# Two unused 64-byte buffers around the activations' low and high halves, in a two-layer decoder trunk on one core

## The chip, the core and the metric

The kernel runs on one core of one Trainium2 chip. The metric is the device time of one execution in microseconds (us); lower is better. A core has TensorE (PE for its matmuls, PEld for its weight loads), VectorE (DVE), ScalarE (ACT), GpSimd (POOL) and SyncE (SP, which here only issues DMAs), one on-chip memory of 128 partitions (SBUF) that all of them read, and PSUM, which holds the matmuls' sums.

## The reference

`x` is 256 tokens by 2048 features, float32. Two layers run one after the other, each followed by a SwiGLU feed-forward block of 5632 hidden features:

```python
c_act = silu(c)
for i in range(2):
    sh1, sc1, g1, sh2, sc2, g2 = split(c_act @ ada_w[i] + ada_b[i], 6)
    h = x * (1 + sc1) + sh1
    y = mixer_ab(h, ...) if i == 0 else mixer_cd(h, ...)
    x = layer_norm(ALPHA * x + (1 + g1) * y, ln1_g[i], ln1_b[i])
    h = x * (1 + sc2) + sh2
    y = (silu(h @ w_gate[i]) * (h @ w_up[i])) @ w_down[i]
    x = layer_norm(ALPHA * x + (1 + g2) * y, ln2_g[i], ln2_b[i])
```

`mixer_ab` is one input projection (2048 to 5136), gated DeltaNet heads beside S5 state-space groups, and an output projection; `mixer_cd` is an input projection (2048 to 6144), a short gated convolution beside differential attention, and an output projection. All weights are float32 and are read once from HBM, about 612 MB in all.

## The kernel before

**Products.** Every large matrix product is cut into weight units of 512 rows by 512 columns (1 MB). SP loads a unit into one of four slots of `w_raw` (line 896 issues it). ACT writes its rounded high part into `w_hi` (line 978), DVE subtracts to get the rest into `w_lo` (line 1262), each with two slots. The activations of a product are split the same way into two buffers: `act_hi` and `act_lo` for all products but the down projections, which take `hid_hi` and `hid_lo`. TensorE then runs three matmuls for each 128 rows: high times high, low times high, high times low, in the format fp32r.

**Two shapes.** In the narrow form (lines 1749, 1751, 1753) a 128x128 block of the weights is what TensorE loads as its stationary operand and 128x256 of the activations streams past it. The products `in0u`, `in0`, `glu`, `out0`, `in1a`, `in1b`, `out1` run so with `act_hi`/`act_lo`, 124 units; the down projections run so with `hid_hi`/`hid_lo`, 88 units. A unit is 16 blocks and 48 matmuls. In the wide form (lines 1741, 1743, 1745) a 128x128 block of the activations is stationary and 128x512 of the weights streams. The gate and up projections run so with `act_hi`/`act_lo`, 176 units of 24 matmuls. The narrow lines:

```python
pe.matmul(dst, whi[:, j % 2, kk, cols], hi[:, k], ...)
pe.matmul(dst, whi[:, j % 2, kk, cols], lo[:, k], ...)
last = pe.matmul(dst, wlo[:, j % 2, kk, cols], hi[:, k], ...)
```

**Order.** The products follow one another on all engines in the order `in0u`, `in0`, `glu`, then the DeltaNet rounds, `out0`, a layer norm, three pairs of up and down blocks, a layer norm, `in1a`, `in1b` (with the attention between its units), `out1`, a layer norm, three pairs of up and down blocks, a last layer norm. Beside them DVE sums the products `c_act @ ada_w` (line 1249) out of units that POOL's or SP's queue loads into `ada_units`; the last of these belongs to the first block of the second layer's up projection.

**Buffers.** `sb(name, shape)` takes the next free bytes of every partition, in the order of the lines, so a buffer's address is the sum of the sizes ahead of it. `shared([...])` takes space and gives it back at once, so that what comes next lies over it: `ada_first` (49152 bytes in each partition), used only at the start, lies over `w_lo`, `act_hi` and `act_lo`. The sizes in bytes of each partition, in order: `w_raw` 32768, `w_hi` 16384, `ada_units` 16384, `ada_acc` 4096, `xT` 16384, `w_lo` 16384, `act_hi` 16384, `act_lo` 16384, then from `mod` to `dn_small` 16 small buffers (columns of vectors, `ident`, `ones`, small weights) of 5824 together, then `y` 16384, `hid_hi` 16384, `hid_lo` 16384, `gate_t`, `gate_s`, `ln_stat`, and over the same space from `y` on the buffers of the S5, DeltaNet and attention stages.

```python
raw = sb("w_raw", [P, 4, UK, GROUP])
whi = sb("w_hi", [P, 2, UK, GROUP], F32R)
aw = sb("ada_units", [P, 2, UK, GROUP])
acc = sb("ada_acc", [P, 2, GROUP])
xT = sb("xT", [P, KT, L])
wlo = sb("w_lo", [P, 2, UK, GROUP], F32R)
ahi = sb("act_hi", [P, KT, L], F32R)
alo = sb("act_lo", [P, KT, L], F32R)
```

Of the kernel before, what the change touches and what calls it, by code (L numbers as in the profile page):

```python
# [12 lines left out]
P = 128  # L13
# [106 lines left out]
def build(nc, x, c, ada_w, ada_b, ln1_g, ln1_b, ln2_g, ln2_b, ffn_w_gate, ffn_w_up, ffn_w_down,  # L120
# [10 lines left out]
    with ctx:  # L131
        def sb(name, shape, dt=F32):
            return ctx.enter_context(nc.sbuf_tensor(name, shape, dt))
# [4 lines left out]
        def shared(layout):  # L138

            with ExitStack() as s:  # L140
                return [s.enter_context(nc.sbuf_tensor(n, shape, F32 if not dt else dt[0])) for n, shape, *dt in layout]
# [7 lines left out]

        (first6,) = shared([("ada_first", [P, FIRST_SLOTS - 2, UK, GROUP])])  # L150
        wlo = sb("w_lo", [P, 2, UK, GROUP], F32R)
        ahi = sb("act_hi", [P, KT, L], F32R)
        alo = sb("act_lo", [P, KT, L], F32R)
        mod = sb("mod", [P, DEPTH * N_ADA])
        adab = sb("ada_b_cols", [P, DEPTH * N_ADA])
        lnc = sb("ln_cols", [P, 4 * DEPTH * KT])
# [1873 lines left out]
```

## Time and profile before

| | us |
|---|---|
| median of 3 runs | 2971.28 |
| lowest and highest | 2968.68, 2972.24 |
| the profiled execution, its own time | 2971.53 |
| its span, first to last instruction | 2968.1 |

Over the span PE is busy 89%, its weight loads 80%, DVE 71%, ACT 40%, POOL 8%; the mean granted clock is 0.914 of full speed. A profile row gives the time from the start of the span in us; a busy share says how long an engine was occupied, not that it ran at its peak: matmuls are pipelined, so one that is listed with 0.28 us may be followed by the next after 0.12 us. The rate is therefore read from the starts.

### The profile page before, as it was taken

The page shows a single profiled execution, that of the slowest core. Times are in us where ns is not written, and L with a number is a line of the kernel's source. Part 1 is how long each engine was busy: PE and PEld are TensorE (multiplying, and loading weights), DVE is VectorE, ACT ScalarE, POOL GpSimd, SP SyncE. Part 2 cuts the span into 40 slices and gives each one's busy share as a digit, 9 for nine tenths or more (in the row PEclk, how much of TensorE's full clock was granted, in tenths as well). Part 3 has the DMA queues.
Part 4 walks back from the last instruction along what each step waited for, and adds up shares of the span by engine and source line. Part 5 has one row for each costly group of instructions (what it writes and reads, how often), then busy time and mean ns, then how long its engine had stood idle before and what let it go on. Part 6 is the DMA issues. An engine that isn't in the chain of part 4 may idle for free.

```text
span 2968.1 us, 43237 instructions
## 1 busy us (share of the span) xinstructions
PE 2640.9 (89%) x16620; PEld 2373.7 (80%) x16620; DVE 2116.8 (71%) x2742; ACT 1200.1 (40%) x1509; POOL 233.2 (8%) x274
## 2 busy tenths in 40 slices
PE   1299999566679899999999989999889999999998
PEld 1298887455569788988898889999878898889887
DVE  7778887666668777777777788756887755555556
ACT  0135554322214544334434445355345434443444
POOL 0012221111120000000000101100000000000000
PEclk6599999665569999999999999999999999999998
DMA  9853333122347488788778859945657755555552
GB/s 339 274 199 114 120 122 119 66 99 99 113 149 275 161 285 284 269 278 285 279 271 281 286 182 324 335 151 169 243 172 270 268 191 192 190 192 189 195 184 85
DMA packets 288724, 615.90 MB, mean 208 GB/s; under 512 B 22572, under 2 KB 23107, under 8 KB 288323
## 3 DMA queue, kind: packets, MB, share of 16 engines
q1 hardware_dynamic: 253762, 479.64, 47.7%
q0 software_dynamic: 34816, 134.23, 12.9%
q8 instruction: 103, 1.69, 0.2%
q14 instruction: 43, 0.34, 0.0%
HBM read 611.73 MB, written 2.10 MB: 207 GB/s over the span
## 4 chain that ended last, share of the span: by engine, by line
PE 76%; issue 11%; DVE 7%; POOL 2%; ACT 1%; DMA 1%; SPq 1%; DVEq 0%; POOLq 0%; ACTq 0%
PE groups L1749 13%; PE groups L1753 12%; PE groups L1751 12%; PE groups L1741 11%; PE groups L1745 10%; PE groups L1743 10%; PE pc L1918 2%; DVE ada_acc L1249 1%; PE pm L1716 1%; PE pb L1907 1%; POOL dn_mb L620 1%; SPq L896 1%; DVE w_lo L1262 1%; DMA ada_units<-in_ada_w_dram 1%; DVE ada_acc L1591 1%
## 5 line engine op out<-in xcount | busy, mean ns | idle before, releaser
L1262 DVE TENSOR_TENSOR w_lo<-w_raw,w_hi 128x1024 fp32r<-128x1024 f32 x773 | 938.5, 1223 | 575.6 <-ACT w_hi L978 571.6
L978 ACT ACTIVATE w_hi<-w_raw 128x1024 fp32r<-128x1024 f32 x776 | 817.5, 1059 | 1262.0 <-PE groups L1753 600.0
L1749 PE MATMUL groups<-act_hi,w_hi 128*128 128x256 f32 x1968 | 572.3, 291 | 43.1 <-DVE act_lo L1392 13.3
L1741 PE MATMUL groups<-w_hi,act_hi 128*128 128x512 f32 x1408 | 554.5, 394 | 25.5 <-DVE act_lo L1392 25.5
L1751 PE MATMUL groups<-act_lo,w_hi 128*128 128x256 f32 x1968 | 563.8, 286 | 0.0
L1753 PE MATMUL groups<-act_hi,w_lo 128*128 128x256 f32 x1968 | 563.5, 286 | 0.0
L1745 PE MATMUL groups<-w_lo,act_hi 128*128 128x512 f32 x1408 | 550.6, 391 | 0.0
L1743 PE MATMUL groups<-w_hi,act_lo 128*128 128x512 f32 x1408 | 550.4, 391 | 0.0
L1249 DVE SCALAR_TENSOR_TENSOR ada_acc<-ada_units,c_act,ada_acc 128x512 f32<-128x512 f32 x600 | 468.2, 780 | 26.3 <-DMA ada_units<-in_ada_w_dram 9.1
L1749 PEld LDWEIGHTS groups<-act_hi,w_hi 128*128 128x128 f32 x1968 | 385.2, 196 | 56.2 <-issue 39.8
L1749 PE MATMUL groups<-hid_hi,w_hi 128*128 128x256 f32 x1392 | 388.1, 279 | 0.0
L1753 PE MATMUL groups<-hid_hi,w_lo 128*128 128x256 f32 x1392 | 386.7, 278 | 0.0
L1751 PE MATMUL groups<-hid_lo,w_hi 128*128 128x256 f32 x1392 | 386.7, 278 | 0.0
L1751 PEld LDWEIGHTS groups<-act_lo,w_hi 128*128 128x128 f32 x1968 | 385.3, 196 | 0.2
L1753 PEld LDWEIGHTS groups<-act_hi,w_lo 128*128 128x128 f32 x1968 | 384.7, 195 | 0.0
L1741 PEld LDWEIGHTS groups<-w_hi,act_hi 128*128 128x128 f32 x1408 | 266.2, 189 | 82.2 <-DVE act_lo L1392 28.0
L1745 PEld LDWEIGHTS groups<-w_lo,act_hi 128*128 128x128 f32 x1408 | 265.8, 189 | 55.9
L1743 PEld LDWEIGHTS groups<-w_hi,act_lo 128*128 128x128 f32 x1408 | 266.3, 189 | 54.6
L1751 PEld LDWEIGHTS groups<-hid_lo,w_hi 128*128 128x128 f32 x1392 | 262.7, 189 | 0.1
L1749 PEld LDWEIGHTS groups<-hid_hi,w_hi 128*128 128x128 f32 x1392 | 261.6, 188 | 0.1
L1753 PEld LDWEIGHTS groups<-hid_hi,w_lo 128*128 128x128 f32 x1392 | 261.7, 188 | 0.0
L889 POOL DMA_DIRECT2D ada_units<-in_ada_w_dram x128 | 96.2, 751 | 1585.1 <-DVE ada_acc L1249 1443.8
(385 smaller groups left out, 2251.5 us busy)
## 6 DMA issues: line engine op xcount, KB each, us to landing
ada_units<-in_ada_w_dram POOLq DMA_DIRECT2D x128, 1024.0 KB, 6.4
w_raw<-in_ffn_w_gate_dram SPq DMA_DIRECT2D x88, 1024.0 KB, 5.2
w_raw<-in_ffn_w_up_dram SPq DMA_DIRECT2D x88, 1024.0 KB, 5.2
w_raw<-in_ffn_w_down_dram SPq DMA_DIRECT2D x88, 1024.0 KB, 5.1
w_raw<-in_cd_w_in_dram SPq DMA_DIRECT2D x48, 1024.0 KB, 6.0
ada_units<-in_ada_w_dram SPq DMA_DIRECT2D x40, 1024.0 KB, 5.1
w_raw<-in_ab_w_in_dram SPq DMA_DIRECT2D x40, 1024.0 KB, 5.0
ada_first<-in_ada_w_dram SPq DMA_DIRECT2D x24, 1024.0 KB, 9.5
```

Source lines behind the costliest of these rows:

```text
L620: done(pool.tensor_tensor(mb[:], m[:], lm[:, k].unsqueeze(1).broadcast_to([P, 4, P]), ALU.mult))
L889: engine.dma_start(aw[:, j % 2], src[UK * P * j:UK * P * (j + 1), bass.ds(col, GROUP)] .rearrange("(k p) n -> p k n", p=P)).then_inc(lande ...
L978: act.activation(whi[:, half, k], raw[:, slot, k], ACT.Copy).then_inc(hi_done, 1)
L1249: last = dve.scalar_tensor_tensor(acc[:, b], unit[:, kk], cact[:, k:k + 1], acc[:, b], ALU.mult, ALU.add)
L1262: dve.tensor_tensor(wlo[:, half, k], raw[:, slot, k], whi[:, half, k].bitcast(F32), ALU.subtract).then_inc(lo_done, 1)
L1741: pe.matmul(dst, hi[:, k, rows], whi[:, j % 2, kk], start=(k == 0), stop=False, skip_group_check=True)
L1743: pe.matmul(dst, lo[:, k, rows], whi[:, j % 2, kk], start=False, stop=False, skip_group_check=True)
L1745: last = pe.matmul(dst, hi[:, k, rows], wlo[:, j % 2, kk], start=False, stop=(k == UK * p["units"] - 1), skip_group_check=True)
L1749: pe.matmul(dst, whi[:, j % 2, kk, cols], hi[:, k], start=(q == 0 and kk == 0 and n % 2 == 0), stop=False, skip_group_check=True)
L1751: pe.matmul(dst, whi[:, j % 2, kk, cols], lo[:, k], start=False, stop=False, skip_group_check=True)
L1753: last = pe.matmul(dst, wlo[:, j % 2, kk, cols], hi[:, k], start=False, stop=(q == p["units"] - 1 and kk == UK - 1), skip_group_check=True)
L1918: last = pe.matmul(pc[cols, 0:L], s5w[:, t, 2 + m, cols], turned[:, c], start=(m == 0 and c == 0), stop=(m == 1 and c == 1))
```

## The change

Two buffers of 16 float32 in each partition are allocated and never written or read. `act_gap` stands ahead of `act_hi`, `act_end` behind `act_lo`. No instruction, wait, loop or transfer is added or removed.

```diff
         wlo = sb("w_lo", [P, 2, UK, GROUP], F32R)
+        sb("act_gap", [P, 16])
         ahi = sb("act_hi", [P, KT, L], F32R)
         alo = sb("act_lo", [P, KT, L], F32R)
+        sb("act_end", [P, 16])
         mod = sb("mod", [P, DEPTH * N_ADA])
```

So `act_hi` and `act_lo` lie 64 bytes further on, and `mod` and all that follows it, `y`, `hid_hi` and `hid_lo` among them, 128 bytes. The buffers from `w_raw` to `w_lo` stay where they are.

## Rows read from the trace of the kernel before

**Rows 1.** Top of the page: span, busy time and share of each engine.

```profile
span 2968.1 us, 43237 instructions
PE 2640.9 (89%) x16620; PEld 2373.7 (80%) x16620; DVE 2116.8 (71%) x2742; ACT 1200.1 (40%) x1509; POOL 233.2 (8%) x274
```

**Rows 2.** The chain that ended last, shares of the span by engine, by line.

```profile
PE 76%; issue 11%; DVE 7%; POOL 2%; ACT 1%; DMA 1%; SPq 1%; DVEq 0%; POOLq 0%; ACTq 0%
PE groups L1749 13%; PE groups L1753 12%; PE groups L1751 12%; PE groups L1741 11%; PE groups L1745 10%; PE groups L1743 10%; PE pc L1918 2%; DVE ada_acc L1249 1%; PE pm L1716 1%; PE pb L1907 1%; POOL dn_mb L620 1%; SPq L896 1%; DVE w_lo L1262 1%; DMA ada_units<-in_ada_w_dram 1%; DVE ada_acc L1591 1%
```

**Rows 3.** Groups of instructions: shapes, count | busy us, mean ns | idle before.

```profile
L1749 PE MATMUL groups<-act_hi,w_hi 128*128 128x256 f32 x1968 | 572.3, 291 | 43.1 <-DVE act_lo L1392 13.3 <-DVE act_lo L1511 11.1 <-DVE act_lo L1675 7.3
L1741 PE MATMUL groups<-w_hi,act_hi 128*128 128x512 f32 x1408 | 554.5, 394 | 25.5 <-DVE act_lo L1392 25.5
L1749 PE MATMUL groups<-hid_hi,w_hi 128*128 128x256 f32 x1392 | 388.1, 279 | 0.0
...
L1262 DVE TENSOR_TENSOR w_lo<-w_raw,w_hi 128x1024 fp32r<-128x1024 f32 x773 | 938.5, 1223 | 575.6 <-ACT w_hi L978 571.6
L1392 DVE TENSOR_TENSOR act_lo<-y,act_hi 128x1024 fp32r<-128x1024 f32 x9 | 11.0, 1221 | 2.4 <-ACT act_hi L1089 2.4
```

**Rows 4.** Timeline of PE, product in1a, narrow form: start, us, instruction; first and last.

```profile
1869.75 0.28 PE L1749 MATMUL groups<-act_hi,w_hi 128*128 128x256 f32 x1
...
1874.91 0.28 PE L1751 MATMUL groups<-act_lo,w_hi 128*128 128x256 f32 x1
```

**Rows 5.** Timeline of PE, up projection, wide form, first and last.

```profile
2499.76 0.39 PE L1745 MATMUL groups<-w_lo,act_hi 128*128 128x512 f32 x1
...
2509.96 0.39 PE L1745 MATMUL groups<-w_lo,act_hi 128*128 128x512 f32 x1
```

**Rows 6.** Timeline of PE, down projection of the second layer, narrow form, first and last.

```profile
2419.74 0.28 PE L1749 MATMUL groups<-hid_hi,w_hi 128*128 128x256 f32 x1
...
2424.95 0.28 PE L1751 MATMUL groups<-hid_lo,w_hi 128*128 128x256 f32 x1
```

**Rows 7.** Timeline of PE, down projection of the first layer, narrow form, first and last.

```profile
1239.73 0.28 PE L1753 MATMUL groups<-hid_hi,w_lo 128*128 128x256 f32 x1
...
1244.91 0.28 PE L1751 MATMUL groups<-hid_lo,w_hi 128*128 128x256 f32 x1
```

**Rows 8.** Timeline of PE, start of in1a, at the granted clock of rows 9, first and last.

```profile
1764.57 0.41 PE L1749 MATMUL groups<-act_hi,w_hi 128*128 128x256 f32 x1
...
1766.49 0.41 PE L1749 MATMUL groups<-act_hi,w_hi 128*128 128x256 f32 x1
```

**Rows 9.** Stretches: length, busy us of each engine (instructions), granted clock, DMA share, GB/s.

```profile
1764.50:1767.00 2.50, 2.50 (x14) 2.50 (x13) 1.67 (x6) 2.08 (x4) 0.00 (x0) 0.50 0.00 0
...
1325.00:1360.00 35.00, 35.00 (x156) 28.97 (x155) 29.31 (x32) 14.81 (x16) 3.00 (x4) 1.00 0.78 265
1870.00:1895.00 25.00, 25.00 (x211) 25.00 (x210) 23.46 (x29) 9.61 (x10) 2.99 (x4) 1.00 1.01 374
...
2400.00:2430.00 30.00, 30.00 (x267) 30.00 (x266) 15.03 (x15) 11.71 (x12) 0.00 (x0) 1.00 0.55 177
2500.00:2520.00 20.00, 20.00 (x90) 16.57 (x89) 9.50 (x8) 8.20 (x8) 0.00 (x0) 1.00 0.60 203
205.00:495.00 290.00, 284.60 (x1920) 234.03 (x1920) 241.06 (x334) 151.88 (x252) 67.89 (x64) 0.99 0.34 116
1240.00:1270.00 30.00, 30.00 (x258) 30.00 (x257) 23.55 (x27) 11.00 (x11) 2.40 (x4) 1.00 0.83 285
```

**Rows 10.** The chain in order of time inside in1a: start, us, what.

```profile
1844.00 8.08 DMA ada_units<-in_ada_w_dram
...
1855.95 8.20 DMA ada_units<-in_ada_w_dram
```

## Prediction

> **What bounds the kernel now.** I read the top of the page first: PE is busy 89% of the span [rows 1]. The chain that ended last confirms it as the bound: 76% of it is PE, and 68% (13+12+12+11+10+10) are the six matmul lines of the products [rows 2]. Busy time does not give the rate of a pipelined engine, so I read starts. Four stretches, each with PE busy all through at a granted clock of 1.00, that is 2.4 GHz [rows 9]:
>
> - narrow, activations in `act_hi`/`act_lo`: 44 matmuls, so 43 steps in 1874.91-1869.75 = 5.16 us, 120.0 ns each [rows 4];
> - wide, same activations: 46 matmuls, 45 steps in 10.20 us, 226.7 ns [rows 5];
> - narrow, `hid_hi`/`hid_lo`: 47 matmuls, 46 steps in 5.21 us, 113.3 ns [rows 6];
> - the same in the first layer: 45 matmuls, 44 steps in 5.18 us, 117.7 ns [rows 7].
>
> At 2.4 GHz 256 columns take 106.7 ns and 512 take 213.3. So a matmul with `act` costs 13.3 ns beyond its columns in either shape, though the shapes differ twofold in length and swap which operand is loaded and which streams. With `hid` it costs 6.7 or 11.0. At a granted clock of 0.50 (1.2 GHz) [rows 9] 10 matmuls of the narrow form with `act` stand 1.92/9 us = 213.3 ns apart, exactly 256 columns [rows 8]: there nothing is added. The excess is a cost of feeding the array at full speed, with one weight load to each matmul, and it depends on which buffer holds the activations. The readers of `act` and `hid` run the same three lines with the same waits.
>
> **What differs between act and hid: the address.** From the sizes, `act_hi` lies 16384+16384+4096+16384+16384 = 69632 bytes behind `w_hi`, a whole number (136) of 512 bytes; rows, blocks and slots of both are multiples of 512 apart, so the loaded and the streamed operand always start on the same place of 512 bytes. `hid_hi` lies 69632+32768+5824+16384 = 124608 behind `w_hi`, 243 times 512 and 192. With 192 = 128+64, `hid` is not on the same place of any 128 bytes. `w_lo` is a multiple of 512 from `w_hi`, and the low halves are 16384 from the high ones.
>
> **The change, part by part.** It adds no instruction and no transfer; all it can do is through these distances. `act` moves from 0 to 64 (modulo 512) and `hid` from 192 to 320. Modulo 128 that is 0 to 64 for `act`, and 64 before and after for `hid`. If two streams that start on the same place collide most, and the pattern repeats every 128 bytes, `act` comes to where `hid` is and `hid` stays.
>
> Price of a matmul: `hid` runs at 113.3 or 117.7 ns [rows 6, 7], 6.7 or 2.3 below 120.0. I take the middle, 4.5, where `act` runs long undisturbed, since `hid` shows both in just such stretches. Bounds are 0 and 6.7.
>
> - Narrow with `act`: 3x1968 = 5904 matmuls [rows 3]. I take off some 250, an estimate, for the runs at 1.2 GHz behind pauses, like that of [rows 8], where nothing is added. `in1a` has 1152 of them at 374 GB/s and a DMA share of 1.01 [rows 9], and its chain already waits twice for `ada_units` [rows 10]: a faster PE waits there for DMA, so I take 0. That leaves 4500. Of these `in0` and `in1b` (56 units, 2688) are cut up, a unit or two at a time, by the S5 and attention matmuls between them; in 205 to 495 us PE's 1920 matmuls are `in0`'s 1536 and 384 others [rows 9]. Here I take the smaller 2.3, since nothing shows what such short pieces settle to: 6.2 us. The other 1800 at 4.5: 8.1 us. Together 14.3 us; bounds 0 and 30.
> - Wide: 3x1408 = 4224 matmuls [rows 3], in long runs. The excess is the same 13.3 ns there, so I take the same 4.5: 19.0 us; bounds 0 and 28.2. The trace has no wide matmul at another distance, so this is the less certain half. What could cap it: a unit of 24 would take 5.32 us instead of 5.44. DVE, busy 29.31 of 35 us [rows 9], and DMA at 265 to 285 GB/s [rows 9] both have more room than the 2% needed.
> - Down projections: 4176 matmuls, 0. If half of them run at 117.7 now and all fell to 113.3, that would give 2088 x 4.3 = 9 us; that is a bound.
> - DVE and ACT: `w_lo` (operands 32768 apart, 0 modulo 512) takes 1223 ns, `act_lo` (operands not on the same place) 1221 for the same elements [rows 3]. So addresses cost DVE nothing, and I take nothing for all moved buffers, vector columns and `ada_first` (in place) included. Waits in layer norms, DeltaNet and attention stay as they are.
>
> Sum: 14.3+19.0 = 33.3 us. The profiled execution took 2971.5 us, 2968.1 of span and 3.4 around it, and is 0.2 from the median shown. 2971.5-33.3 = 2938.
>
> The Trainium skill speaks against any of this: "TensorE: Matmul & The Clock Gate", section "Step-by-step: what each phase is for", says that PE has two independent read ports, so that loading the next weights takes no read bandwidth from the running matmul, and "SBUF — State Buffer", section "Who interferes with whom", that PE waits on nobody. By that the distances would not matter and the time stays at 2971. The first page's section "Back-to-back issue gap" gives N/2.4 + 2.5 ns for one matmul alone, 109.2 and 215.8; the trace is above both with either buffer, by rows 4 to 7.
>
> **The rivals.**
>
> *Nothing moves (2971).* Rows 6 and 7 have the same lines, shape and addresses and still differ by 4.3 ns, so a part of the spacing comes from how loads and matmuls fall into step, not from addresses. If the remaining difference to `act` is also that, or if the pattern repeats every 64 bytes (both 0 and 192 are then the same), the change is nothing. Against it: the difference of buffer goes one way in every pair of [rows 4] against [rows 6, 7], and the wide form, with other lengths and the operands swapped, has the same 13.3 ns [rows 5] as the narrow [rows 4].
>
> *Only one shape gains.* Narrow alone: 2971.5-14.3 = 2957. Wide alone: 2971.5-19.0 = 2952. For it: which operand moves is swapped, so a distance of +64 is -64 in the other shape.
>
> *Only the step at 117.7 is reached.* 2.3 ns on 8724 matmuls: 20 us, 2951.
>
> *Slower: hid loses its place (2990).* If the pattern is longer than 128 bytes, 320 modulo 512 need not be as good as 192. Should the down projections take `act`'s 120.0 while `act` keeps its own, 4176 x 4.5 ns = 19 us are added. It decides as soon as `hid` loses more than `act` gains: at a loss of 4.5 on `hid`, when `act` gains less than 19 us / 8724 = 2.2 ns a matmul. The like for `act`, a distance worse than the same place, has no row for it; doubled to 6.7 more it would cost 58 us.
>
> **How the numbers follow.** Both shapes gain, 2904 to 2951: 0.45. Only one gains, 2952 to 2957: 0.15. Nothing: 0.20. Slower: 0.17. The rest, 0.03, is a small gain near 2963. The range reaches from the best bound (30+28.2+9 = 67, 2904, cut to 2910, since that needs every matmul at its best) to 2973, just past no change, which leaves out the slower cases. The likeliest case alone is 2912 to 2951. 0.2% is 6 us, about what a measurement of this kernel can tell from no change: faster 0.62, same 0.21, slower 0.17.
>
> **What the next profile would show.** Right: spacing of the narrow form in `in1b`, `out1` and of the wide form falls from 120.0 and 226.7 to 113-118 and 220-224, with `hid` as before and the counts of [rows 3] unchanged; `in1a` as long as before, with more DMA in its chain; durations on DVE and ACT unchanged. Wrong: `act` at 120.0 and 226.7 as before, or the down projections' stretches [rows 6, 7] at 120. The step I trust least is the wide form's 4.5 ns.

## The result and the profile after

The changed kernel takes 3003.5 us (median of 4 runs) against 2971.7 (4 runs): ratio 1.0102, interval [1.0088, 1.0117]. It is slower by 1.0%, about 32 us; forecast were 2938 us and a range of 2910 to 2973. The profiled execution has a span of 2999.0 us, 30.9 more than before [rows 1].

Top of the page, then the line of the chain by source line. Two lines were inserted, so a line of before has a number higher by two: L1743, L1745, L1747 are the wide form, L1751, L1753, L1755 the narrow one.

```profile
span 2999.0 us, 43237 instructions
PE 2668.6 (89%) x16620; PEld 2371.6 (79%) x16620; DVE 2116.9 (71%) x2742; ACT 1199.5 (40%) x1509; POOL 233.0 (8%) x274
...
PE groups L1751 12%; PE groups L1753 12%; PE groups L1755 12%; PE groups L1743 11%; PE groups L1745 11%; PE groups L1747 11%; PE pc L1920 2%; DVE ada_acc L1251 1%; PE pm L1718 1%; PE pb L1909 1%; DMA ada_units<-in_ada_w_dram 1%; SPq L898 1%; POOL dn_mb L622 1%; DVE w_lo L1264 1%; DVE ada_acc L1593 1%
```

The instructions are the same in number, DVE and ACT are as busy as before to 0.6 us, the granted clock is 0.914 in both. PE is busy 27.7 us longer. Groups of the page, as in [rows 3]:

```profile
L1264 DVE TENSOR_TENSOR w_lo<-w_raw,w_hi 128x1024 fp32r<-128x1024 f32 x773 | 937.8, 1223 | 604.0 <-ACT w_hi L980 601.9
...
L1751 PE MATMUL groups<-act_hi,w_hi 128*128 128x256 f32 x1968 | 566.1, 288 | 45.3 <-DVE act_lo L1394 13.7
L1743 PE MATMUL groups<-w_hi,act_hi 128*128 128x512 f32 x1408 | 561.8, 399 | 22.0 <-DVE act_lo L1394 22.0
...
L1751 PE MATMUL groups<-hid_hi,w_hi 128*128 128x256 f32 x1392 | 389.9, 280 | 0.0
```

The mean duration of a narrow matmul with `act` fell from 291 to 288 ns, that of a wide one rose from 394 to 399, that with `hid` from 279 to 280. DVE still takes 1223 ns for a piece; its idle time before `w_lo` rose from 575.6 to 604.0 us, nearly all of it (601.9) waiting for ACT, whose own longest wait is for PE. The rate shows in the starts. Four stretches of PE's timeline (start, duration, instruction; first and last), with 45, 44, 45 and 44 matmuls:

```profile
1884.80 0.28 PE L1755 MATMUL groups<-act_hi,w_lo 128*128 128x256 f32 x1
...
1889.98 0.28 PE L1753 MATMUL groups<-act_lo,w_hi 128*128 128x256 f32 x1
...
2519.74 0.39 PE L1747 MATMUL groups<-w_lo,act_hi 128*128 128x512 f32 x1
...
2529.78 0.39 PE L1743 MATMUL groups<-w_hi,act_hi 128*128 128x512 f32 x1
...
2429.77 0.28 PE L1751 MATMUL groups<-hid_hi,w_hi 128*128 128x256 f32 x1
...
2434.95 0.28 PE L1755 MATMUL groups<-hid_hi,w_lo 128*128 128x256 f32 x1
...
1244.84 0.28 PE L1753 MATMUL groups<-hid_lo,w_hi 128*128 128x256 f32 x1
...
1249.90 0.28 PE L1755 MATMUL groups<-hid_hi,w_lo 128*128 128x256 f32 x1
```

- narrow with `act`: 5.18 us / 44 = 117.7 ns, was 120.0 [rows 4];
- wide with `act`: 10.04 / 43 = 233.5, was 226.7 [rows 5];
- `hid`, second layer: 5.18 / 44 = 117.7, was 113.3 [rows 6];
- `hid`, first layer: 5.06 / 43 = 117.7, as before [rows 7].

Where the 31 us went, by the time from the first to the last start of each stretch of products, in both traces:

| products | before, us | after, us | difference |
|---|---|---|---|
| up, six blocks (wide) | 1001.7 | 1026.4 | +24.7 |
| down, six blocks (`hid`) | 495.7 | 507.1 | +11.4 |
| `in0u` to `glu` (narrow, `act`) | 385.7 | 384.1 | -1.6 |
| `out0` (narrow, `act`) | 96.5 | 95.0 | -1.5 |
| `in1a` to `out1` (narrow, `act`) | 423.5 | 418.5 | -5.0 |
| sum | | | +28.0 |

The other 3 us of the 31 lie outside the products: the first one starts 1.4 us later, and the DeltaNet stretch between `glu` and `out0` is 1.6 us longer.

### The profile page after: what moved, and what is told of

The parts are those of the page before. It is cut to its first block, busy times and chain, and to the rows that moved or that the text cites. A ratio compares the mean times of both kernels' runs of the same rounds, so it can differ in the third digit from the quotient of the medians.

```text
span 2999.0 us, 43237 instructions
## 1 busy us (share of the span) xinstructions
PE 2668.6 (89%) x16620; PEld 2371.6 (79%) x16620; DVE 2116.9 (71%) x2742; ACT 1199.5 (40%) x1509; POOL 233.0 (8%) x274
## 4 chain that ended last, share of the span: by engine, by line
PE 77%; issue 11%; DVE 7%; POOL 1%; ACT 1%; DMA 1%; SPq 1%; DVEq 0%; POOLq 0%; ACTq 0%
PE groups L1751 12%; PE groups L1753 12%; PE groups L1755 12%; PE groups L1743 11%; PE groups L1745 11%; PE groups L1747 11%; PE pc L1920 2%; DVE ada_acc L1251 1%; PE pm L1718 1%; PE pb L1909 1%; DMA ada_units<-in_ada_w_dram 1%; SPq L898 1%; POOL dn_mb L622 1%; DVE w_lo L1264 1%; DVE ada_acc L1593 1%
## 5 line engine op out<-in xcount | busy, mean ns | idle before, releaser
L1264 DVE TENSOR_TENSOR w_lo<-w_raw,w_hi 128x1024 fp32r<-128x1024 f32 x773 | 937.8, 1223 | 604.0 <-ACT w_hi L980 601.9
L1751 PE MATMUL groups<-act_hi,w_hi 128*128 128x256 f32 x1968 | 566.1, 288 | 45.3 <-DVE act_lo L1394 13.7
L1743 PE MATMUL groups<-w_hi,act_hi 128*128 128x512 f32 x1408 | 561.8, 399 | 22.0 <-DVE act_lo L1394 22.0
L1745 PE MATMUL groups<-w_hi,act_lo 128*128 128x512 f32 x1408 | 558.3, 397 | 0.0
L1747 PE MATMUL groups<-w_lo,act_hi 128*128 128x512 f32 x1408 | 558.1, 396 | 0.0
L1753 PE MATMUL groups<-act_lo,w_hi 128*128 128x256 f32 x1968 | 557.5, 283 | 0.0
L1755 PE MATMUL groups<-act_hi,w_lo 128*128 128x256 f32 x1968 | 557.2, 283 | 0.0
L1751 PEld LDWEIGHTS groups<-act_hi,w_hi 128*128 128x128 f32 x1968 | 378.4, 192 | 58.4 <-issue 42.0
L1751 PE MATMUL groups<-hid_hi,w_hi 128*128 128x256 f32 x1392 | 389.9, 280 | 0.0
L1753 PE MATMUL groups<-hid_lo,w_hi 128*128 128x256 f32 x1392 | 389.7, 280 | 0.0
L1755 PE MATMUL groups<-hid_hi,w_lo 128*128 128x256 f32 x1392 | 388.4, 279 | 0.0
L1753 PEld LDWEIGHTS groups<-act_lo,w_hi 128*128 128x128 f32 x1968 | 378.5, 192 | 0.2
L1755 PEld LDWEIGHTS groups<-act_hi,w_lo 128*128 128x128 f32 x1968 | 377.9, 192 | 0.0
L1743 PEld LDWEIGHTS groups<-w_hi,act_hi 128*128 128x128 f32 x1408 | 265.8, 189 | 88.5 <-DVE act_lo L1394 24.5
L1747 PEld LDWEIGHTS groups<-w_lo,act_hi 128*128 128x128 f32 x1408 | 265.6, 189 | 66.0
L1745 PEld LDWEIGHTS groups<-w_hi,act_lo 128*128 128x128 f32 x1408 | 265.8, 189 | 63.6
L1751 PEld LDWEIGHTS groups<-hid_hi,w_hi 128*128 128x128 f32 x1392 | 261.7, 188 | 0.1
L1753 PEld LDWEIGHTS groups<-hid_lo,w_hi 128*128 128x128 f32 x1392 | 261.3, 188 | 0.1
L1755 PEld LDWEIGHTS groups<-hid_hi,w_lo 128*128 128x128 f32 x1392 | 260.4, 187 | 0.0
```

The costliest lines, as they stand in the source:

```text
L1264: dve.tensor_tensor(wlo[:, half, k], raw[:, slot, k], whi[:, half, k].bitcast(F32), ALU.subtract).then_inc(lo_done, 1)
L1743: pe.matmul(dst, hi[:, k, rows], whi[:, j % 2, kk], start=(k == 0), stop=False, skip_group_check=True)
L1745: pe.matmul(dst, lo[:, k, rows], whi[:, j % 2, kk], start=False, stop=False, skip_group_check=True)
L1747: last = pe.matmul(dst, hi[:, k, rows], wlo[:, j % 2, kk], start=False, stop=(k == UK * p["units"] - 1), skip_group_check=True)
L1751: pe.matmul(dst, whi[:, j % 2, kk, cols], hi[:, k], start=(q == 0 and kk == 0 and n % 2 == 0), stop=False, skip_group_check=True)
L1753: pe.matmul(dst, whi[:, j % 2, kk, cols], lo[:, k], start=False, stop=False, skip_group_check=True)
```

## The experiments

The theory that I tested, D: the distance between the buffer of the activations and the buffers of the weights, modulo some period, sets the spacing of the product's matmuls. Rivals: what else moved (S), the place in the memory itself (A), chance of timing (P). The kernels of experiments 1 to 12 and 16 are the one before with unused buffers of other sizes; "act at 64" means 64 bytes more than before between `w_hi` and `act_hi`, and `hid` is named by its distance modulo 512. Beside each timeline I give a mean: the mean spacing over all neighbouring matmuls of that kind in the trace, without pauses and without stretches at 1.2 GHz (over 5400 narrow with `act`, over 4100 with `hid`, over 4000 wide), in the order narrow with `act`, `hid`, wide; it is good to about 0.1 ns. For the kernel before these means are 119.9, 115.0 and 226.8, for the changed one 117.4, 117.8 and 233.3.

**1. The buffers behind alone.**

```diff
         alo = sb("act_lo", [P, KT, L], F32R)
+        sb("act_end", [P, 32])
```

> act stays at distance 0 (modulo 512) from w_hi, hid and all small buffers move 128 bytes as in the changed kernel. Theory D (the distance of an activation buffer from the weights' buffers sets the spacing of its own matmuls): hid at 117.7 ns in all stretches, act at 120.0 and 226.7 as before; 4176 x 2.8 ns = +12 us, about 2983 us. Theory S (the moved small buffers, or the program as a whole, slow it): the wide form loses its 6.6 ns here too, about 3000 us. Theory P (the spacing is how loads and matmuls fall into step by chance of timing): nothing, 2971 us.

Measured 1.0036 [1.0018, 1.0054], 2981.4 us. `hid` at 320, then the wide form:

```profile
2419.78 0.28 PE L1752 MATMUL groups<-hid_lo,w_hi 128*128 128x256 f32 x1
...
2424.96 0.28 PE L1750 MATMUL groups<-hid_hi,w_hi 128*128 128x256 f32 x1
...
2499.76 0.39 PE L1744 MATMUL groups<-w_hi,act_lo 128*128 128x512 f32 x1
...
2509.96 0.39 PE L1744 MATMUL groups<-w_hi,act_lo 128*128 128x512 f32 x1
```

45 matmuls in 5.18 us are 117.7 ns where [rows 6] had 113.3; 46 in 10.20 us are 226.7, as before. The means are 119.9, 117.3, 226.9. `hid` slows when it moves by itself, by about a third of the whole loss (down blocks 505.0 us, 9.3 more than before), though not in all stretches: in two of the six blocks 4 of 11 pieces of 48 steps still stood at 113.3. S falls for the wide form.

**2. act alone.**

```diff
+        sb("act_gap", [P, 16])
         ahi = sb("act_hi", [P, KT, L], F32R)
         alo = sb("act_lo", [P, KT, L], F32R)
+        sb("act_end", [P, 112])
```

> act at distance 64, hid at 192+512 = 704, which is 192 modulo 512. Theory D with a period of 512 or less: act as in the changed kernel (117.7 narrow, 233.3 wide), hid as before the change (113.3 and 117.7, mean 115.0); -12+28 = +16 us, about 2987 us. If hid stays at 117.7 throughout, the period is longer than 512 or hid's state is not its distance: about 2999 us.

1.0109 [1.0086, 1.0131], 32 us by the ratio (26 by the medians) against the 16 forecast for an undisturbed `hid`; it is the other branch, 2999 us, that came. 45 wide matmuls took 10.27 us, 233.4 ns, and 45 of `hid` 5.18 us, 117.7 ns, where [rows 6] had 113.3:

```profile
2509.64 0.39 PE L1743 MATMUL groups<-w_hi,act_hi 128*128 128x512 f32 x1
...
2519.91 0.39 PE L1747 MATMUL groups<-w_lo,act_hi 128*128 128x512 f32 x1
...
2429.74 0.28 PE L1753 MATMUL groups<-hid_lo,w_hi 128*128 128x256 f32 x1
...
2434.92 0.28 PE L1751 MATMUL groups<-hid_hi,w_hi 128*128 128x256 f32 x1
```

The means are 117.8, 117.1, 233.3. `act` behaves as in the changed kernel. But `hid`, at its old distance, ran at 117.7 most of the time: the down blocks took 504.6 us, 8.9 more than before, nearly as much as in experiment 1. So at 192 it has two states, 113.3 and 117.7, and which one holds is not given by its distance. As both also occur at 320 (experiment 1), the two distances differ for `hid` in how often each state holds, not in the values.

**3. Both 512 further on** (`act_gap` of 128 elements, no other).

> act and hid both move 512 bytes, so both keep their place modulo 512. Theory D with a period of 512 or less: no change, 2971 us, 120.0, 226.7 and 115.0 ns. Theory S: as slow as the changed kernel, about 3000 us. If the pattern is longer than 512 bytes, the spacings move in some way.

0.9999 [0.9986, 1.0012]; means 119.9, 114.5, 226.8. Nothing changed, so the period divides 512. S falls with experiments 1 and 2: in 2 the small buffers moved by the same 512 bytes and the wide form slowed, in 1 they moved by the change's 128 and it did not.

**4. act at 192, hid at 384** (`act_gap` of 48 elements).

> act at distance 192, where hid was before; hid at 384. Theory D: the narrow form with act takes hid's spacing of before, 113.3 or 117.7 ns (mean 115.0), 5 ns x some 4500 = -22 us; the wide form has the distance -192 and no row says what it costs: 226.7 as at 0 gives about 2950 us, 233.3 as at 64 gives about 2977 us; hid at 384 unknown, 113 to 120. Theory P: act at 120.0 as before.

1.0024 [1.0011, 1.0038], about 7 us slower: the narrow form as expected, the sum not (2981.2 us by the median against 2950 or 2977). Wide, 45 matmuls in 10.07 us, 228.9 ns:

```profile
2504.77 0.39 PE L1744 MATMUL groups<-w_hi,act_lo 128*128 128x512 f32 x1
...
2514.84 0.39 PE L1742 MATMUL groups<-w_hi,act_hi 128*128 128x512 f32 x1
```

The means are 115.4 (`act` took on what `hid` had at 192), 118.7 and 229.1.

**5. Everything 64 further on, distances kept.**

```diff
+        sb("front_gap", [P, 16])
         raw = sb("w_raw", [P, 4, UK, GROUP])
```

> 64 unused bytes ahead of w_raw: every buffer moves 64 bytes and all distances between them stay. Theory D (distance between the operands): 120.0, 226.7 and about 115 ns as before, 2971 us. Theory A (the place of the activations itself in the memory, not their distance from the weights): as act moved by 64, wide at 233.3, narrow at 117.7, about 2990 us or more.

1.001 [0.9995, 1.0025]; 46 wide matmuls in 10.20 us, 226.7 ns; means 119.9, 114.5, 226.8.

```profile
2499.79 0.39 PE L1746 MATMUL groups<-w_lo,act_hi 128*128 128x512 f32 x1
...
2509.99 0.39 PE L1746 MATMUL groups<-w_lo,act_hi 128*128 128x512 f32 x1
```

Theory A falls: the distance counts, not the place. The distance to what is less sure. `w_raw`, `w_hi`, `ada_units`, `xT` and `w_lo` kept their distances from one another in every kernel, so no run tells the weights' buffers, which TensorE reads, from the others, which ACT, DVE and DMA use. That the weights' buffers are the partner is argued from the trace: in [rows 5] every one of the 45 steps took 226 or 227 ns, though DVE was busy for only 9.50 of 20 us there and ACT for 8.20 [rows 9]. What slows each matmul alike must be there for each, as the weight loads are.

**6. act_lo alone by 64** (16 elements between `act_hi` and `act_lo`, 112 behind).

> Only act_lo moves by 64 bytes, act_hi stays at 0, hid keeps 192 modulo 512. Theory D, pair by pair (what streams against what is being loaded meanwhile): one of the three intervals of a triple changes, a third of the effect: narrow 120.0 - 0.8 = 119.2, wide 226.7 + 2.2 = 228.9, about 2971 - 4 + 9 = 2976 us. Rival, the triple locks as a whole: the narrow and wide means stay at 120.0 and 226.7 or go all the way to 117.7 and 233.3.

1.0065 [1.0046, 1.0084], 18 us by the medians instead of the 5 forecast. The wide mean is 231.1, two thirds of the way to 233.3, not one. By the place in the triple, the wide intervals are 229.2, 235.5 and 228.5. So the wide triple does not go as a whole, but a pair is not simply the matmul and the next load either: a move of one low operand reached all three intervals. The narrow mean is 119.0, but as a mixture: in 14 of the 15 pieces of 48 steps of `out0` it stood at 117.8, in 29 of the 61 pieces from `in1a` to `out1` at 119.9 or 120.0. There the rival, a triple that goes as a whole, describes it better. My expectation was wrong in both shapes, and which accesses meet stays open.

**7 and 8. act at 448 and at 320** (`act_gap` of 112 and 80 elements, `act_end` of 16 and 48).

> act at distance 448, which is -64 modulo 512; hid at 192 modulo 512. Theory D with the sign counted as streamed minus loaded: the narrow form at -64, which is what the wide form had in the changed kernel, costs 6.6 ns more (20.0 beyond its columns, 126.7), and the wide form at +64 costs 2.3 less (224.3): 4500 x 6.6 - 4224 x 2.3 = +20 us, about 2991 us. Rival, the sign does not count and each shape has its own cost of being off the same place: narrow 117.7, wide 233.3, about 2989 us: the times are near, the spacings tell.

> act at distance 320, where hid was in the changed kernel; hid at 192 modulo 512. Theory D: narrow 117.8 or less, as hid showed there; the wide form at -320, which is +192 modulo 512. If the sign counts as streamed minus loaded, it takes the excess that the narrow form had at +192 (6.7 or 11.0): 220 to 224 ns, so 2971 - 10 - 4224 x (2.3 to 6.7), about 2933 to 2952 us. If the sign does not count: 229 ns as at distance 192, about 2972 us.

At 448: 0.9996 [0.9983, 1.0009]; means 115.1, 117.4, 229.2. At 320: 1.0085 [1.0053, 1.0118]; means 117.8, 116.8, 233.3. The wide form at 448 (46 matmuls in 10.30 us, 228.9 ns), then at 320 (45 in 10.26 us, 233.2 ns):

```profile
2494.69 0.39 PE L1745 MATMUL groups<-w_hi,act_lo 128*128 128x512 f32 x1
...
2504.99 0.39 PE L1745 MATMUL groups<-w_hi,act_lo 128*128 128x512 f32 x1
```

```profile
2514.68 0.39 PE L1743 MATMUL groups<-w_hi,act_hi 128*128 128x512 f32 x1
...
2524.94 0.39 PE L1747 MATMUL groups<-w_lo,act_hi 128*128 128x512 f32 x1
```

Both of my readings of the sign missed: the times were 2971.5 us at 448 against 2989 or 2991, and 2998.4 at 320 against at most 2972. What fits is simpler: 448 is as 192, and 320 as 64, in both shapes. That is a period of 256.

**9 to 12. act at 256, 128, 32 and 224**, `hid` at 192.

> act at distance 256, hid at 192 modulo 512. So far act at 64 and at 320 gave the same spacings (117.7 and 233.3), and act at 192 and at 448 too (113 to 118 and 229). Theory D256 (the pattern repeats every 256 bytes): act at 256 is act at 0, 120.0 and 226.7 ns, about 2971 us. Theory D512 (only every 512): other spacings than at 0.

> act at distance 128, hid at 192 modulo 512. My forecast's assumption, a repeat every 128 bytes, says 120.0 and 226.7 as at 0; it already fails on act at 64 against 192. Theory D256: a value of its own; hid at 384, which is 128 modulo 256, ran at 118.7 narrow, so 118.7 here; wide unknown, between 226.7 and 233.3: 2966 to 2994 us.

> act at distance 32, half of the change's step; hid at 192 modulo 512. If the cost comes from equal lines of 64 bytes or more, 32 acts as 0: 120.0 and 226.7, 2971 us. If it is finer than that, it is between 0 and 64 (118 to 119, 230) or has a value of its own: 2975 to 2985 us.

> act at distance 224, which is -32 modulo 256; hid at 192 modulo 512. If 32 bytes less than a whole period acts as 0: 120.0 and 226.7. If it acts as 192: 115 and 229, 2960 to 2971 us. A finer pattern has a value of its own; this one and act at 32 together say whether the sign of a small distance counts.

At 256: 1.0 [0.9987, 1.0014], 226.7 ns for 46 wide matmuls: as at 0, the period is 256. At 128: 1.0091 [1.0067, 1.0115]; at 32: 1.0056 [1.0038, 1.0074], with 44 wide matmuls in 10.04 us, 233.5 ns; at 224: 1.0079 [1.0055, 1.0103]. The times of these three missed: 128 took 3000.1 us, above the range up to 2994; 32 took 2987.3, and neither acted as 0 nor lay between 0 and 64; 224 took 2991.5 and acted neither as 0 nor as 192. The sign of a small distance counts in the narrow form (116.8 at 32, 118.3 at 224) and not in the wide one (233.3 at both). The wide form of the kernels with `act` at 256, then at 32:

```profile
2499.74 0.39 PE L1743 MATMUL groups<-w_hi,act_hi 128*128 128x512 f32 x1
...
2509.94 0.39 PE L1743 MATMUL groups<-w_hi,act_hi 128*128 128x512 f32 x1
```

```profile
2504.82 0.40 PE L1745 MATMUL groups<-w_hi,act_lo 128*128 128x512 f32 x1
...
2514.86 0.40 PE L1747 MATMUL groups<-w_lo,act_hi 128*128 128x512 f32 x1
```

The mean spacings by distance modulo 256, all kernels but that of experiment 6 together:

| distance | narrow, `act` | narrow, `hid` | wide, `act` |
|---|---|---|---|
| 0 | 119.9 | 120.0 | 226.8 to 226.9 |
| 32 | 116.8 | | 233.3 |
| 64 | 117.4 to 117.8 | 117.3 to 117.8 | 233.3 |
| 128 | 118.9 | 118.7 | 232.7 |
| 192 | 115.0 to 115.4 | 114.4 to 117.4 | 229.1 to 229.2 |
| 224 | 118.3 | | 233.3 |

The spread of `hid` at 192 has an order. In the kernels with the wide products, which run before each down block, at 0, 32, 128 or 224 its mean was 114.4 to 115.6; with the wide products at 64 or 192 it was 116.8 to 117.4. So the state of a stretch follows what ran before it. Each mean is of one profiled execution, and how the state is passed on stays open.

**13 to 15. The two shapes apart.** One room for each half, used at one offset by the narrow products and at another by the wide ones; the up projections and the layer norms that write for them take `ahw`, `alw`. A room is 256 bytes longer than its buffer, so all other distances stay as they were modulo 256:

```diff
-        ahi = sb("act_hi", [P, KT, L], F32R)
-        alo = sb("act_lo", [P, KT, L], F32R)
+        act_room = [sb(n, [P, KT * L + 64], F32R) for n in ("act_hi", "act_lo")]
+        def placed(at):
+            return [room[:, at // 4:at // 4 + KT * L].rearrange("p (k l) -> p k l", l=L) for room in act_room]
+        (ahi, alo), (ahw, alw) = placed(192), placed(0)
...
-                    product(up, on_act(2 * layer + 1), after=turned,
+                    product(up, on_act(2 * layer + 1), ahw, alw, after=turned,
```

This is experiment 13. The other two kernels have `placed(0), placed(64)` (14) and `placed(64), placed(0)` (15), and come first here.

> The change's distance for the wide products alone: narrow at 0, wide at 64, hid at 192 modulo 512. Theory D256: narrow 119.9, wide 233.3, hid 114.5 to 117.5: 4224 x 6.5 = +27 us, 2999 us, the whole of the changed kernel's loss and a little more. Rival (what slows is something that all matmuls share): narrow or hid change too.

1.0121 [1.0102, 1.014]: the wide form's part alone, with what follows from it, costs 36 to 37 us. 44 wide matmuls took 10.04 us, 233.5 ns; 44 narrow ones of `in1a` 5.16 us, 120.0:

```profile
2519.73 0.39 PE L1750 MATMUL groups<-w_lo,act_hi 128*128 128x512 f32 x1
...
2529.77 0.39 PE L1746 MATMUL groups<-w_hi,act_hi 128*128 128x512 f32 x1
...
1899.74 0.28 PE L1754 MATMUL groups<-act_hi,w_hi 128*128 128x256 f32 x1
...
1904.90 0.28 PE L1756 MATMUL groups<-act_lo,w_hi 128*128 128x256 f32 x1
```

The means are 119.9, 117.4, 233.3. The up blocks are 24.5 us longer than before; the down blocks 10.0 us, since `hid` at an unchanged 192 was mostly in its slower state. The cost is more than the 27 us forecast by about that.

> The change's distance for the narrow products alone: narrow at 64, wide at 0, hid at 192 modulo 512. Theory D256: narrow 117.5 to 117.8, wide 226.8: -12 us, 2960 us, if the narrow products turn every ns into time; -8 or less if waits take some of it back.

0.9985 [0.9972, 0.9997]; means 117.8, 114.7, 226.8. The narrow part of the change is a gain, but of 4 us (1 to 8 by the interval) against the 12 forecast; it lies in the branch "-8 or less if waits take some of it back". In the profiled execution the narrow products with `act` were 7.5 us shorter, the DeltaNet stretch 1.2 longer.

> One room for the activations, used at distance 192 by the narrow products and at 0 by the wide ones; hid at 192 modulo 512. Theory D256: narrow 115, wide 226.8 ns; in0 and the other narrow products gain 4.6 ns on some 4500 matmuls, -20 us at most and about -15 with what in1a and the waits keep: 2950 to 2960 us, faster than both kernels. If the shapes can't be had apart (the state carries over from product to product), wide goes to 229 and the time to 2965 to 2980 us.

0.9932 [0.9917, 0.9947], 2950.9 us (5 runs) beside 2972.8: faster by 20 us (0.0068 of 2972.8) than the kernel before beside it, and about 52 below the changed kernel's median. 46 wide matmuls in 10.20 us are 226.7 ns; 46 narrow ones of `out0` in 5.10 us are 113.3:

```profile
2474.76 0.39 PE L1746 MATMUL groups<-w_hi,act_hi 128*128 128x512 f32 x1
...
2484.96 0.39 PE L1746 MATMUL groups<-w_hi,act_hi 128*128 128x512 f32 x1
...
939.80 0.28 PE L1754 MATMUL groups<-act_hi,w_hi 128*128 128x256 f32 x1
...
944.90 0.28 PE L1754 MATMUL groups<-act_hi,w_hi 128*128 128x256 f32 x1
```

The means are 115.0, 114.7, 226.9, in the table the best of each shape at once. The stretch of `out0` shows the lower of the narrow form's two values at 192; 6 of its 15 pieces of 48 steps stood at 117.8, hence the mean.

**16. hid at act's old distance** (`act_end` of 16 elements, nothing else).

> act stays at 0 for both shapes; hid at 256, which is 0 modulo 256. Theory D256, for any buffer: hid takes the 120.0 ns that act has at 0 in the same shape, 4176 x 5 = +21 us, about 2992 us. Rival (the buffer or what runs beside it makes the difference, not the distance): hid stays at 113 to 118.

1.008 [1.0065, 1.0094], 2994.0 us. 44 matmuls in 5.16 us, 120.0 ns, mean 120.0, against 113.3 in [rows 6]:

```profile
2429.76 0.28 PE L1750 MATMUL groups<-hid_hi,w_hi 128*128 128x256 f32 x1
...
2434.92 0.28 PE L1752 MATMUL groups<-hid_lo,w_hi 128*128 128x256 f32 x1
```

Another buffer, other products, the same number at the same distance: for the narrow form D holds for both pairs of buffers tried.

## Why the prediction was wrong

**The bound** was read rightly: PE sets the pace, and spacing turns into time. 6.5 ns on 4224 wide matmuls are 27 us by the means, 24.7 by the lengths of the blocks. The sums hold, but for one rounding: a unit of 24 at 222.2 ns is 5.33 us, not 5.32.

**"What differs between act and hid: the address"** was right as to the distance (experiments 3, 5 and 16), but not the whole: `hid` has two states at one distance, and which holds follows what runs before it. DVE's total busy time stayed at 2116.8 and 2116.9 us, so the moved addresses cost it nothing, as assumed. The Trainium skill says that loading the next weights takes no read bandwidth from the running matmul ("TensorE: Matmul & The Clock Gate", section "Step-by-step: what each phase is for"). The prediction drew from it that the distances would not matter; for these fp32r matmuls they do, 226.7 or 233.3 ns for the same instructions, and the measurement decides. Whether it is the read ports that meet, no run shows.

**The step that failed: "the pattern repeats every 128 bytes, `act` comes to where `hid` is and `hid` stays".** The rows gave two distances, 0 and 192, and I chose the period that made the new distances old ones. The period is 256: `act` went to 64, which no row showed, and `hid` from 192 to 64 too. The down blocks lost 11.4 us where I had put 0. The rival "hid loses its place" (0.17) had `hid` slow down, but at 120.0 and with `act` as before; it ran at 117.7. Nor was its place the only cause. `hid` moved alone costs the down blocks 9.3 us (experiment 1), but `act` moved alone costs them 8.9 (2), and the wide products moved alone 10.0 (14). Either move is enough for most of the 11.4, and the two do not add; so I was also wrong to price the down projections by their own distance alone.

**The step that failed worse: "The excess is the same 13.3 ns there, so I take the same 4.5: 19.0 us".** The two shapes do have the same excess at distance 0, and at no other measured one. The wide form rises by 2.3 at 192 and by about 6.5 at 32, 64 and 224 and by 5.9 at 128; of all distances tried 0 is its best and, for the narrow form, 0 is the worst. The term was -19.0 and measured +24.7. I had called it the less certain half and still bounded it at 0 from below, with no reason that excluded a loss; the "+58 us" for a worse distance stood as a remark and not as a bound of the range. Nor did the signs of being wrong name a wide form at 233.3.

**The narrow term** had the right sign: -14.3 forecast, -8.2 by the lengths. The long stretches settled at 117.7 and not midway, but the short pieces and `in1a` took that spacing too, so that the means promise 14 us (2.5 ns on 5600 neighbours). The rest was taken back: in these products the pauses grew by 3.6 us in total, and some 20 more matmuls ran at the spacing of 1.2 GHz, 2 us. `in1a`, for which I had put 0, became 1.6 us shorter (153.7 us, now 152.1).

## What to carry to other kernels

Where PE is the bound and its operands come from different buffers, read the spacing of the starts for each pair of buffers and shape: some ns between pairs that should be equal are whole per cents. Treat the distance between the operands as a parameter, one for each shape, and try it in steps within 256 bytes (the period that these two shapes showed here); it costs no instruction, and in this kernel the worst and the best placement tried are 2% apart (1.0121 and 0.9932). Look at the products behind the one that was moved, too: the down blocks lost 10.0 us in experiment 14 with their own operands at the old distances modulo 512. Two samples of a periodic effect don't give its period, and a value for one shape isn't one for another.

## What the runs showed of the hardware

- The spacing of fp32r matmuls, one weight load to each, depends on the distance of the two operands' buffers modulo 256 bytes at the 2.4 GHz level: 113.3 to 120.0 ns for 256 columns, 226.7 to 233.5 for 512, with the weights' buffers as the likely partner (see experiment 5). At 1.2 GHz it was 213 or 214 for 256 and 426 or 427 for 512 in most steps of the traces of all 18 kernels, whatever the distance, with nothing added (213.3 in [rows 8]).
- It keeps exact steady values (113.3, 117.7, 120.0; 226.7) for hundreds of matmuls and then may take another at the same distance: `hid` at 192 had a mean from 114.4 to 117.4 in different kernels, 117.4 in the one of experiment 14, which moved only the wide products, and both 113.3 and 117.7 occur at 64 as at 192. The distance of the wide products that ran before changed which is more frequent; how a stretch enters its state stays open, as does what inside the memory or PE collides: only spacings were seen.
